# Slot scatters four deep instead of two, and the slot table turned one unit of gate products earlier, in a hybrid decoder layer with 64 experts

## The reference

```python
h = layer_norm(DN_ALPHA * h + mix, ln1_g[l], ln1_b[l])
ffn = moe(h, router_w[l], router_b[l], exp_w_gu[l], exp_w_down[l], sh_w_gu[l], sh_w_down[l])
ple = jax.nn.sigmoid(h @ ple_w_g[l] + ple_b_g[l]) * (p[l].astype(h.dtype) @ ple_w_e[l])
h = layer_norm(DN_ALPHA * h + ffn + ple, ln2_g[l], ln2_b[l])

def moe(x, router_w, router_b, exp_w_gu, exp_w_down, sh_w_gu, sh_w_down):
    ...
    _, eidx = lax.top_k(jnp.where(emask, sel, -jnp.inf), TOP_K)
    ...
    routed = routed_experts(xt, eidx, gw, exp_w_gu, exp_w_down)
    shared = swiglu(xt, sh_w_gu, sh_w_down)
    return (routed + shared).reshape(b, s, d)
```

## Time and profile before

| | us |
|---|---|
| median of 3 runs | 2316.85 |
| the three runs | 2315.64, 2316.85, 2322.55 |
| the profiled execution | 2325.7 |
| its span in the trace | 2323.9 |
| PE busy | 2261.9 (97%) |
| DVE, ACT, POOL busy | 1162.8, 465.3, 758.0 |

### The profile page before, as it was taken

How to read it: one execution, slowest core, us unless ns; L and a number is a source line. 1 busy time by engine, 2 the same in 40 slices (tenths; PEclk the granted TensorE clock), 3 DMA queues, 4 the chain that set the end, 5 groups by cost and what they waited for, 6 DMA issues and landing times.

```text
span 2323.9 us, 26832 instructions
## 1 busy us (share of the span) xinstructions
PE 2261.9 (97%) x9664; PEld 1331.3 (57%) x9664; DVE 1162.8 (50%) x2027; ACT 465.3 (20%) x779; POOL 758.0 (33%) x756
## 2 busy tenths in 40 slices
PE   9999999999999999999999999999999999999995
PEld 5784554445894444444445477665666656565653
DVE  7543887887646445555764755222222222223225
ACT  3001125655331110111012100111111111111113
POOL 1000110003520000000000356567676675766652
PEclk9999999999999999999999999999999999999998
DMA  8111001122012111010605013999999998999975
GB/s 311 61 57 53 26 11 60 55 73 74 3 44 75 55 64 55 30 52 28 227 37 208 23 55 118 343 354 363 331 345 321 331 350 286 350 313 351 328 250 180
DMA packets 142581, 386.12 MB, mean 166 GB/s; under 512 B 22700, under 2 KB 51616, under 8 KB 141426
## 3 DMA queue, kind: packets, MB, share of 16 engines
q1 hardware_dynamic: 110258, 307.49, 35.8%
q0 software_dynamic: 31152, 70.09, 11.9%
q10 hardware_dynamic: 1040, 6.83, 0.7%
HBM read 328.86 MB, written 66.58 MB: 170 GB/s over the span
## 4 chain that ended last, share of the span: by engine, by line
PE 90%; DVE 4%; issue 2%; DMA 1%; ACT 1%; POOL 0%; another core or an unknown queue 0%; POOLq 0%; SPq 0%; DVEq 0%; ACTq 0%
PE banks L2678 13%; PE banks L1916 12%; PE banks L2686 9%; PE banks L2723 9%; PE banks L465 6%; PE banks L1928 6%; PE banks L1139 5%; PE banks L2520 4%; PE banks L2626 3%; PE banks L512 3%; PE banks L2505 2%; PE banks L340 2%; PE banks L1151 2%; PE banks L2614 1%; PE banks L2701 1%
## 5 line engine op out<-in xcount | busy, mean ns | idle before, releaser
L2678 PE MATMUL banks<-arena 128*128 128x136 f32 (+8 forms) x2240 | 325.5, 305 | 22.6 <-issue 22.4
L3405 POOL DMA_INDIRECT arena<-hp_scratch,arena x300 | 305.2, 1017 | 101.4 <-issue 90.7
L2678 PEld LDWEIGHTS banks<-arena 128*128 128x128 f32 x2240 | 315.2, 196 | 32.4 <-issue 32.4
L1916 PE MATMUL banks<-arena 128*128 128x512 f32 x672 | 290.5, 592 | 0.0
L2686 PE MATMUL banks<-arena 128*128 128x512 f32 (+1 forms) x528 | 237.6, 592 | 0.3 <-ACT arena L2863 0.3
L1916 PEld LDWEIGHTS banks<-arena 128*128 128x128 f32 x672 | 127.2, 189 | 160.1 <-issue 160.1
L2723 PE MATMUL banks<-arena 128*128 128x512 f32 x464 | 207.1, 598 | 5.3 <-DVE arena L3226 5.3
L3421 POOL DMA_INDIRECT acc_scratch<-arena x97 | 150.6, 1553 | 151.0 <-DVE arena L3299 61.5
L286 POOL TENSOR_SCALAR arena<-arena 128x1 f32<-128x1 f32 x16 | 4.9, 306 | 562.7 <-DVE arena L277 562.7
L3226 DVE STREAM_TRANSPOSE arena<-arena 128x1024 f32<-128x1024 f32 (+3 forms) x97 | 96.2, 999 | 158.4 <-DMA arena<-gt_scratch,arena 149.2
L2686 PEld LDWEIGHTS banks<-arena 128*128 128x128 f32 (+1 forms) x528 | 97.3, 188 | 111.3 <-issue 110.0
(11 more groups left out here) (480 smaller groups left out, 2990.4 us busy)
## 6 DMA issues: line engine op xcount, KB each, us to landing
arena<-in_exp_w_gu SPq DMA_DIRECT2D x64, 2048.0 KB
arena<-in_exp_w_down SPq DMA_DIRECT2D x64, 1024.0 KB
arena<-in_w_in SPq DMA_DIRECT2D x22, 1024.0 KB, 5.5
arena<-in_w_in SPq DMA_DIRECT2D x5, 2048.0 KB, 7.8
arena<-in_w_branch SPq DMA_DIRECT2D x12, 512.0 KB, 6.5
arena<-in_ple_w_g SPq DMA_DIRECT2D x3, 2048.0 KB
hp_scratch<-arena SPq DMA_DIRECT2D x10, 512.0 KB, 3.1
acc_scratch<-arena SPq DMA_DIRECT2D x10, 512.0 KB, 4.5
```

The source lines that it names most:

```text
L1916: last = nc.tensor.matmul(PS[:, g % 4, :], lhs[:, k, :], rhs[:, k, :], start=(k == 0), stop=(k == 3))
L2678: last = nc.tensor.matmul(PS[:, bank + part, f * n:(f + 1) * n], weights[:, k, part * FF + f * P:part * FF + (f + 1) * P], x[:, k, 0:n], s ...
L3405: nc.gpsimd.indirect_dma_start(out=rows[0:n, :], out_offset=None, in_=table, in_offset=bass.IndirectOffsetOnAxis(ap=at, axis=0), bounds_ch ...
```

## The change

Two numbers and what follows from them. The scatters take four semaphores in turn, and scatter i waits for scatter i - 4; SP waits for 16 scatters on each of the four. `SLOTS_AT` goes from 5 to 4 (units count from 0), so that PE's turning and DVE's integers stand one unit earlier.

```diff
-SLOTS_AT = 5
+SLOTS_AT = 4
+SCATTERS = 4
...
-            e_slots = [sem(f"e_slots{i}") for i in range(2)]
+            e_slots = [sem(f"e_slots{i}") for i in range(SCATTERS)]
...
-                for i in range(2):
-                    sp.wait_ge(e_slots[i], 8 * NT * TOPK)
+                for done in e_slots:
+                    sp.wait_ge(done, 16 * NT * TOPK // SCATTERS)
...
-                        if i >= 2:
-                            pool.wait_ge(e_slots[i % 2], 16 * (i // 2))
+                        if i >= SCATTERS:
+                            pool.wait_ge(e_slots[i % SCATTERS], 16 * (i // SCATTERS))
                         nc.gpsimd.indirect_dma_start(
                             out=slot_d, out_offset=bass.IndirectOffsetOnAxis(ap=pos_i[:, i:i + 1], axis=0),
-                            in_=tok_id[:, t:t + 1], in_offset=None).then_inc(e_slots[i % 2], 16)
+                            in_=tok_id[:, t:t + 1], in_offset=None).then_inc(e_slots[i % SCATTERS], 16)
```

## The result

The changed kernel is slower: 2336.58 us in the median of five runs (2334.84 to 2343.44), against 2316.85 us for the kernel before (2312.94 to 2322.55 in five). The ratio is 1.0095, with a 95% interval of 1.0077 to 1.0113. The forecast was 2315.9, and the range ended at 2321.5. The profiled execution took 2336.22 us (span 2334.4).

The account below looks back on a forecast made before the run. TensorE (PE) was taken to bound the kernel, holding 90% of the chain. Only 1.0 us, from the second place's rows coming earlier, was counted: 2316.85 - 1.0 = 2315.9 us, range 2308.2 to 2321.5.

Parts of the forecast that it names:

- Four in flight: POOL's slot scatters: landing waits shrink from 27.5 to 2.2 us, last scatter ends at 1403.6 instead of 1422.13.
- The tail and the turning: After the last scatter: table ready at 1408.8, PE's turning after unit 4 covered by 3.8 us, at worst costing 1.2.
- the third rival: Scatters don't come home in time, PE stands before the turning: 2324.7 to 2333.9 us; chance 0.09.
- The gathers and the weights: POOL's 14 gathers end near 1434 instead of 1449.74; SP's second-place weights go at about 1407; 1.0 us gained before the experts.
- the second rival: PE's late signals move to the gathers below unit 5, stopping PE 3.2 us plus 2.3 for the clock: 2317 to 2322; 0.09.
- POOL is waited for by nobody while it scatters: During the slot scatters no engine waits for POOL; SP is queued behind it.
- the late signals come sooner: PE's late signals fall in unit 5, up to 8.4 us late, stopping PE 3.2 us plus 2.3 clock; chance 0.09.
- Two of three ordinary runs don't have the hole: PE's loss before the first expert product, 7.63 us, was taken as mostly absent from ordinary runs, so not counted as gain.
- the hole: PE's 5.29 us idle before the first expert product plus slower products after it, 7.63 us in all, 0.33% of the time.
- The first rival: PE's 7.63 us loss before the first expert product is in ordinary runs too and goes: 2309.2 us; chance 0.25.
- The rule on what a queue of two can hide: For POOL's scatters: fixed cost some 2.0 us each, so two in flight (2.52 us) would always hide the landing.

Follow-up runs that it names:

- e2: The changed kernel with two scatters in flight instead of four, table still turned after unit 4: 2327.05 us, 1.0045 of the kernel before.
- e1: The changed kernel with the table turned after unit 5 as before, four scatters still in flight: 2351.03 us, 1.0156 of the kernel before.
- e7: The changed kernel, table turned after unit 5, POOL clearing an unused tile (1.55 us) before each eighth scatter: 2313.80 us, 0.9988 of the kernel before.
- e10: The kernel before, with POOL clearing a small tile (0.15 us) ahead of every place's gathers: 2314.28 us, 1.0000.
- e8: The changed kernel, table turned after unit 5, all earlier scatters landed before each eighth: 2315.04 us, 0.9986 of the kernel before.
- e15: The kernel before, with about 1.2 us of unread arithmetic on POOL before every second place's gathers: 2313.45 us, 0.9965.
- e14: The changed kernel, table turned after unit 5, scatters of 64 partitions instead of 128: 2371.91 us in one run, comparable with no other time.
- e12: The changed kernel with a 1.55 us clearing on POOL before each sixteenth scatter: 2324.75 us, 1.0041 of the kernel before.
- e9: The changed kernel with a 0.17 us clearing on POOL before each eighth scatter: 2338.19 us, 1.0093 of the kernel before.
- e13: e7 with one more pause of about 1.2 us on POOL, between the first two places' gathers: 2320.28 us, 0.9990 of the kernel before.
- e16: e7 with POOL pauses between the first two places' gathers and before every second place's: 2314.04 us, 0.9967 of the kernel before.

## Why the prediction was wrong

*Four in flight: right.* The last scatter ends at 1406.8, and the whole stretch starts 1.6 us later in this execution (1315.38 against 1313.78), which makes 1405.2 for the 1403.6 of the sum (1402.6 to 1408.6). The two waits left cost 7.5 us, at the upper end of 7.2 and not the 2.2 that I took; the scatters themselves were some 3 us shorter.

*The tail and the turning: right.* From the last scatter's end to the copy's end it is 5.66 us (5.16), the table is ready at 1412.4, and PE doesn't wait for it. On the old place of the units in time, unit 4 would have ended at 1412.62 + 1.6 = 1414.2, so the cover was 1.8 us. e2 shows the price where it is missing, 14.68 us, as the third rival had it.

*The gathers and the weights: wrong, as a consequence.* The gathers run from 1445.1 to 1463.4 and not before 1434, because the units in front of them are late. The second place's weights go at 1426.29 and not at 1407: in the program they also wait for unit 3's last product, and that is late too. The 14 gathers again lie beside late signals, now below the products of unit 5, where the second rival had put them:

```profile
1460.78 0.42 DVE L3208 TENSOR_TENSOR arena<-arena,banks 128x256 f32<-128x256 f32 x1 [2.18 <-DMA y_lru_scratch<-arena]
1464.32 0.42 DVE L3208 TENSOR_TENSOR arena<-arena,banks 128x256 f32<-128x256 f32 x1 [3.13 <-PE banks L2627]
```

These are the adds of its sixth and seventh product, done by 1456.9 and 1458.6, so they are 4 and 6 us late. PE doesn't stop there. At that place the rival's price of 3.2 us came to nothing; its mechanism struck elsewhere.

*"POOL is waited for by nobody while it scatters": this is the step that failed.* It is true of every semaphore in the program and was read from the views of waits. But POOL's transfers touch PE without a semaphore. I had the mechanism, as the rival "the late signals come sooner", and mis-sized it in three ways. It was put below the gathers of unit 5, not below the scatters. It was priced by the one case at hand, a signal 8.4 us late at the end of a run of 14, as if that were a ceiling: 3.2 + 2.3 us. The measured loss is 27.0, at the end of 38. And it got 0.09, because I saw no reason for the late signals and took them for an accident of that place. The reason stood in the rows: all scatters without a wait before them are 1.26 us apart, and the 24 landing waits, which I counted only as cost, were the pauses that kept the scatters' runs at 8 or 9. The late signals of the earlier trace rows begin some 10 us into the only longer run so far, the 14 gathers of the earlier trace rows. Taking the waits away joins 38 scatters, and that could have been read off as well.

*"Two of three ordinary runs don't have the hole": most likely wrong.* Wherever the table is turned after unit 5 and no pause of 1 us or more parts the first 14 gathers, the profiled execution has the hole: 4.7 us in e1 and e7, 4.8 in e10, 4.9 in e8, 5.2 in e15, 5.3 in e14. What was unusual in the profiled execution of before is the loop: 22.4 us of "issue" before line 2678, where twelve of the other sixteen kernels have 12.6 to 18.1, one has less, two have 19.7 and 19.9 and one 22.9. PE's waits, before and after (in all, times, longest):

```profile
PE banks L2678 <- issue: 22.4, 33, 1.6
PE banks L2723 <- DVE arena L3226: 5.3, 1, 5.3
```
```profile
PE banks L2627 <- issue: 16.6, 2, 15.9
PE banks L2679 <- issue: 12.6, 26, 1.2
PE banks L2635 <- issue: 5.5, 3, 2.2
```

The 15.9 us of "issue" before line 2627 are the stop in which PE waited for DVE's token sum. With the hole in ordinary runs the sum closes. Lost in the unit 27.0, won in the hole 7.63: 19.4, against 19.7 between the medians. For the two profiled executions 22.4 - 12.6 = 9.8 us of the loop come off: 9.6, and with the 1.6 us by which this one was late already 11.2, against 10.5. That the hole is in ordinary runs is worked out so and not seen, since only one execution of each kernel is profiled. The first rival was then right that the hole goes; what takes its place costs three and a half times as much.

*The rule on what a queue of two can hide* (the Trainium skill, DMA: Bandwidth & Descriptors, section "Anatomy of one DMA — SWDGE (gpsimd) path"): by an estimate from its fixed cost of some 2.0 us two in flight would always do. e2 has that queue and waits 31 times for landings, 30.4 us in all, so the trace disagrees again. But I had asked only what the landing waits cost, by the rule and by the rows, and not what they did for others.

*What stays open* is what the transfers and PE share. The data packets don't pile up: in the stalled stretch of the changed kernel, 1384 to 1396 us, the software queue moved 289 packets, 32 for each scatter, so nine scatters in 12 us, as fast as they are issued.

```profile
q0 software_dynamic: 289, 0.01, 1.8%
```

Nor do landings, as far as they are recorded: on the first of the four semaphores they come in at 1383.77, 1388.82, 1393.87, 1398.93 and 1404.01, each 5.05 to 5.08 us, which is four scatters (single increments of a landing come up to 1.2 us later, and not all are in the record). DVE's signals reach PE at once (1396.50 to 1396.55). Late are PE's signals to DVE, and PE's own single products from 1405.95 on. It isn't an effect of profiling: the four unprofiled runs of the changed kernel took 2334.84 to 2343.44 us. The runs show that it goes by the spacing and the length of a run of transfers, and that about 1.6 us without one in each eight, or 1.2 between the first two places, help; which part of the chip is the narrow one they don't show, and no kernel that would tell (the same spacing with transfers of another kind, or another engine's) was tried.

## What to carry to other kernels

A wait that costs a side engine time can be what spaces its requests; before taking it out, look how long an unbroken run of requests becomes, and whether the trace already has such a run somewhere and what the critical engine did at its end. A late signal without a cause in the profile isn't noise to be given a small chance and a capped price: find what runs beside each case of it, and scale it with that. If a long run of POOL's indirect transfers can't be avoided, about 1.5 us of other work in eight cost nothing clear of the noise here and took the whole loss away (e7).

## What the hardware showed that was not expected

- Indirect transfers of POOL at 1.26 to 1.28 us each delay PE's signals by up to 33 us within a run of 38, with the DMA engines 0.02 busy. With one each 1.36 us the effect is about halved (e12: 13.9 us in two gaps against 30.0 in e9), at 1.45 small (e13: 4.9 us in the units), at 1.52 and more absent (e16, e7, the kernel before).
- When such a run has ended, the signals that were held back come together: four within 0.3 us at 1411.6, for products that were done between 1378.9 and 1402.3.
- In these stretches PE moves in steps of 0.70 us. Single products start 2.80, 2.80 and 2.80 us apart in e14, and 2.80 and 2.10 in the changed kernel (1405.95, 1408.75, 1410.85).
- The second cost of a stop is the clock. In the changed kernel the lower level was granted for 17.0 us from 1383.6, of which PE stood still for 13, and again for 6.8 us from 1407.5, behind the single products: 4.9 of the 27.0 us are slower products.
